# A recurrence kernel on one Trainium2 core: the older wave's products put ahead of the younger wave's in every shared phase

## What is computed

```python
def rwkv7_scan(r, decay, k, v, a, bb, s0):
    def step(s, inp):
        r_t, w_t, k_t, v_t, a_t, b_t = inp
        sa = jnp.einsum('bhij,bhj->bhi', s, a_t)
        s = s * w_t[:, :, None, :] + sa[..., None] * b_t[:, :, None, :] + v_t[..., None] * k_t[:, :, None, :]
        return s, jnp.einsum('bhij,bhj->bhi', s, r_t)
    xs = tuple(jnp.moveaxis(z, 1, 0) for z in (r, decay, k, v, a, bb))
    s, ys = lax.scan(step, s0, xs)
    return jnp.moveaxis(ys, 0, 1), s
```

## Time and profile before

| | us |
|---|---|
| median of three runs | 3079.1 |
| lowest, highest | 3076.35, 3082.09 |
| profiled execution, its time | 3077.25 |
| profiled execution, its span | 3075.1 |
| PE busy | 2827.9 |
| DVE busy | 1222.3 |
| POOL busy | 811.9 |
| ACT busy | 753.4 |

### The profile page before, as it was taken

How to read it: one execution, slowest core, us unless ns; L and a number is a source line. 1 busy time by engine, 2 the same in 40 slices (tenths; PEclk the granted TensorE clock), 3 DMA queues, 4 the chain that set the end, 5 groups by cost and what they waited for, 6 DMA issues and landing times.

```text
span 3075.1 us, 58817 instructions
## 1 busy us (share of the span) xinstructions
PE 2827.9 (92%) x24335; PEld 2689.7 (87%) x24335; DVE 1222.3 (40%) x2402; ACT 753.4 (24%) x1371; POOL 811.9 (26%) x575
## 2 busy tenths in 40 slices
PE   4997777877999999999999999798989999999996
PEld 4997566765799999999999999676989999999996
DVE  6117666675513222121123599974232211121123
ACT  2001344334513121121112310256131111121211
POOL 3212000000162223232236422110532322232345
PEclk9998899998999999999999999899999999999998
DMA  4694000000211111111111211200311111111112
GB/s 123 65 68 54 2 3 3 4 3 20 80 41 38 45 48 40 50 41 43 46 46 36 108 48 41 94 1 4 103 36 36 52 44 45 48 36 53 41 40 74
DMA packets 54003, 138.68 MB, mean 45 GB/s; under 512 B 7248, under 2 KB 23248, under 8 KB 53584
## 3 DMA queue, kind: packets, MB, share of 16 engines
q1 hardware_dynamic: 53840, 136.31, 17.9%
HBM read 119.71 MB, written 16.59 MB: 44 GB/s over the span
## 4 chain that ended last, share of the span: by engine, by line
PE 87%; DVE 8%; ACT 2%; issue 2%; DMA 1%; SPq 0%; ACTq 0%; DVEq 0%; POOLq 0%; POOL 0%
PE PS L319 24%; PE PS L321 24%; PE PS L320 24%; PE PS L1436 3%; PE PS L1387 2%; PE PS L882 1%; PE PS L1462 1%; PE PS L985 1%; DVE zc L1614 1%; PE PS L997 1%; PE PS L935 1%; DVE xx L1316 1%; DVE c_s L1537 1%; DVE h_lo L455 1%; PE PS L1000 1%
## 5 line engine op out<-in xcount | busy, mean ns | idle before, releaser
L319 PE MATMUL PS<-h_hi,w_hi 128*128 128x384 f32 (+1 forms) x3456 | 1135.0, 328 | 63.8 <-POOL w_lo L411 26.3
L320 PE MATMUL PS<-h_lo,w_hi 128*128 128x384 f32 (+1 forms) x3456 | 1132.8, 328 | 0.0
L321 PE MATMUL PS<-h_hi,w_lo 128*128 128x384 f32 (+1 forms) x3456 | 1132.6, 328 | 0.0
L411 POOL TENSOR_TENSOR w_lo<-w_raw,w_hi 128x1024 fp32r<-128x1024 f32 (+2 forms) x208 | 470.2, 2261 | 1113.3 <-ACT w_hi L389 1113.3
L319 PEld LDWEIGHTS PS<-h_hi,w_hi 128*128 128x128 f32 x3456 | 652.8, 189 | 65.0 <-issue 64.7
L320 PEld LDWEIGHTS PS<-h_lo,w_hi 128*128 128x128 f32 x3456 | 652.6, 189 | 0.3
L321 PEld LDWEIGHTS PS<-h_hi,w_lo 128*128 128x128 f32 x3456 | 652.5, 189 | 0.0
L389 ACT ACTIVATE w_hi<-w_raw 128x1024 fp32r<-128x1024 f32 (+2 forms) x208 | 201.8, 971 | 916.5 <-PE PS L321 880.1
L681 DVE TENSOR_TENSOR x<-PS,x 128x384 f32 (+1 forms) x240 | 128.3, 535 | 556.8 <-PE PS L321 551.4
L321 PE MATMUL PS<-hid_hi,w_lo 128*128 128x384 f32 (+1 forms) x1056 | 346.9, 328 | 0.0
L319 PE MATMUL PS<-hid_hi,w_hi 128*128 128x384 f32 (+1 forms) x1056 | 346.7, 328 | 0.0
(11 more groups left out here) (245 smaller groups left out, 2706.4 us busy)
## 6 DMA issues: line engine op xcount, KB each, us to landing
w_raw<-in_w_gu SPq DMA_DIRECT2D x88, 512.0 KB, 3.5
w_raw<-in_w_d SPq DMA_DIRECT2D x48, 384.0 KB, 3.1
w_raw<-in_w_e SPq DMA_DIRECT2D x20, 512.0 KB, 9.0
w_raw<-in_w_o SPq DMA_DIRECT2D x20, 512.0 KB, 3.5
x<-in_x SPq DMA_DIRECT2D x4, 1536.0 KB, 9.1
x_home<-x SPq DMA_DIRECT2D x1, 4352.0 KB, 13.9
w_raw<-in_w_oe SPq DMA_DIRECT2D x8, 512.0 KB, 3.5
w_raw<-in_w_d SPq DMA_DIRECT2D x16, 256.0 KB, 2.7
```

Source lines behind the costliest of these rows:

```text
L319: pe.matmul(out, w_h, a_h, start=k == 0, stop=False)
L320: pe.matmul(out, w_h, a_l, start=False, stop=False)
L321: last = pe.matmul(out, w_l, a_h, start=False, stop=k == kn - 1)
L411: pool.tensor_tensor(w_lo[slot][:, 0:kn, :], w_raw[slot][:, 0:kn, :], w_hi[slot][:, 0:kn, :].bitcast(F32), ALU.subtract).then_inc(sm["w_lo ...
```

## The change

In a mixed phase all products of the back half come ahead of the three `intra`, and the transposes are spread between them. PE: `solved` for both heads, `token_major` 0, `effective`, `token_major` 1, `transfer`, `token_major` 2, `inside`, then `intra` 0, 1, 2. DVE: the `wz` copies, the start state, `r_eff`, `m_all`, then the three reads, `bt_level` and `xx`. ACT: two copies of transposed blocks, `h_all`, the third copy. Every instruction is there as often as before and has the same waits; phases with only one half have the order that they had. No transfer is touched.

```diff
@@ rwkv_act, phase
+                def turned(blk):
+                    act.wait_ge(sm["tm_done"], 3 * qf + (blk + 1))
+                    act.activation(tm[front % 2][blk][:, :, :], PS[:, TM_BANKS[blk], :].rearrange("p (a b) -> p a b", a=4),
+                                   ACT.Copy).then_inc(sm["tm_ready"], 1)
+
                 if front is not None:
-                    for blk in range(WAVE):
-                        act.wait_ge(sm["tm_done"], 3 * qf + (blk + 1))
...
+                    turned(0)
+                    turned(1)
...
                                    ACT.Copy).then_inc(sm["hbd_ready"], 1)
+                if front is not None:
+                    turned(2)
@@ rwkv_pe, phase
                     if back is not None:
                         pe.wait_ge(sm["ysb_ready"], 10 * qb + 10)
-                    token_major(m, front, 0)
-                    token_major(m, front, 1)
                 if back is not None:
                     pe.wait_ge(sm["akv_ready"], qb + 1)
                     solved(back, qb, 0)
-                if front is not None:
-                    token_major(m, front, 2)
-                if back is not None:
                     solved(back, qb, 1)
                 if front is None and m + 1 < PAIRS:
                     decay_low(m + 1)
                 if front is not None:
-                    pe.wait_ge(sm["tm_ready"], 3 * qf + 2)
-                    intra(front, 0)
+                    token_major(m, front, 0)
                 if back is not None:
                     pe.wait_ge(sm["wz_ready"], 2 * qb + 2)
                     pe.wait_ge(sm["y_stored"], qb + 1)
                     effective(back, qb)
                 if front is not None:
-                    pe.wait_ge(sm["tm_ready"], 3 * qf + 3)
-                    intra(front, 1)
+                    token_major(m, front, 1)
                 if back is not None:
                     transfer(back, qb)
                 if front is None and m + 1 < PAIRS:
                     rate_low(m + 1)
                 if front is not None:
-                    pe.wait_ge(sm["sa_ready"], 3 * qf + 1)
-                    intra(front, 2)
+                    token_major(m, front, 2)
                 if back is not None:
                     pe.wait_ge(sm["r_ready"], qb + 1)
                     inside(back, qb)
+                if front is not None:
+                    pe.wait_ge(sm["tm_ready"], 3 * qf + 2)
+                    intra(front, 0)
+                    pe.wait_ge(sm["tm_ready"], 3 * qf + 3)
+                    intra(front, 1)
+                    pe.wait_ge(sm["sa_ready"], 3 * qf + 1)
+                    intra(front, 2)
@@ rwkv_dve, phase
                     ins.then_inc(sm["s_init"], 1)
-                if front is not None:
-                    read_intra(0)
-                if back is not None:
                     dve.wait_ge(sm["reff_done"], qb + 1)
...
                     ins.then_inc(sm["r_ready"], 1)
+                    dve.wait_ge(sm["mh_done"], qb + 1)
+                    dve.wait_ge(sm["mdiag_ready"], qb + 1)
+                    dve.wait_ge(sm["hbd_ready"], qb + 1)
+                    dve.tensor_tensor(m_all[:, :, :].rearrange("p (b a) c -> p b a c", a=2),
+                                      PS[:, 4:6, 0:WAVE * HD].rearrange("p a (b c) -> p b a c", c=HD),
+                                      m_diag[:, :, :].rearrange("p (b a) c -> p b a c", a=2), ALU.add)\
+                       .then_inc(sm["mbd_ready"], 1)
                 if front is not None:
+                    read_intra(0)
                     read_intra(1)
                     read_intra(2)
...
-                if back is not None:
-                    dve.wait_ge(sm["mh_done"], qb + 1)
-                    dve.wait_ge(sm["mdiag_ready"], qb + 1)
-                    dve.wait_ge(sm["hbd_ready"], qb + 1)
-                    dve.tensor_tensor(m_all[:, :, :].rearrange("p (b a) c -> p b a c", a=2),
...
```

More of the change, by code:

```diff
@@ L824, in store_y @@
                     ins.then_inc(sm["y_stored"], 1)
+                def turned(blk):
+                    act.wait_ge(sm["tm_done"], 3 * qf + (blk + 1))
+                    act.activation(tm[front % 2][blk][:, :, :], PS[:, TM_BANKS[blk], :].rearrange("p (a b) -> p a b", a=4),
+                                   ACT.Copy).then_inc(sm["tm_ready"], 1)
                 if front is not None:
-                    for blk in range(WAVE):
-                        act.wait_ge(sm["tm_done"], 3 * qf + (blk + 1))
-                        act.activation(tm[front % 2][blk][:, :, :], PS[:, TM_BANKS[blk], :].rearrange("p (a b) -> p a b", a=4),
-                                       ACT.Copy).then_inc(sm["tm_ready"], 1)
+                    turned(0)
+                    turned(1)
                 if front is None and m + 1 < PAIRS:
@@ L1284, in phase @@
                            .then_inc(sm["x_init"], 1)
-                if back is not None:
-                    dve.wait_ge(sm["mh_done"], qb + 1)
-                    dve.wait_ge(sm["mdiag_ready"], qb + 1)
-                    dve.wait_ge(sm["hbd_ready"], qb + 1)
-                    dve.tensor_tensor(m_all[:, :, :].rearrange("p (b a) c -> p b a c", a=2),
-                                      PS[:, 4:6, 0:WAVE * HD].rearrange("p a (b c) -> p b a c", c=HD),
-                                      m_diag[:, :, :].rearrange("p (b a) c -> p b a c", a=2), ALU.add)\
-                       .then_inc(sm["mbd_ready"], 1)
                 if front is None:
```

## The result

The changed kernel is **slower by a quarter of a per cent**: 3087.39 us against 3079.77 us in the median of 11 runs each, ratio 1.0026 with a 95% interval of 1.0018 to 1.0035, or some 5.5 to 10.8 us. I had forecast 12.4 us; the direction, the place and the range held, the size was too large by about 5 us.

What follows compares the result with a forecast made beforehand. The third read's end sets a mixed phase: PE's list bounds it before, DVE's reads after. M1 1.80 times 4 (7.2) plus M2 1.30 times 4 (5.2) gives +12.4, from 3079.1 to 3091.5 us; range 3083 to 3099.

Steps and rivals of the forecast that it cites:

- The place: Mixed phases: the end of DVE's third read sets the phase's end; level 1 starts 3.69 us behind it.
- The start: Phase start on PE: `solved` waits for the last add before it, `effective` follows 2.26 us later, transpose 0 costs nothing.
- PE from `effective` to the first `intra`: Back half on PE: `effective` 0.40, two transposes 0.65 each, `transfer` 1.05, `inside` 0.70; together 3.45 us.
- The reads: DVE's three reads back to back: first 0.92 us after the first `intra` starts, third ends 2.96 later, 1.80 later than before.
- Stalls ahead of the third read: PE waiting for code in mixed phases: 0.2 us in M1, 0.35 in M2; bounds 0 and 1.1.
- The levels: Behind the third read: lists unchanged; only M1 gains 0.20 us, as the stall ending `inside` no longer holds `values_in`.
- rival A: Loss mostly given back: thinner code stalls in the levels and some worth of `m_all`; +5.8 us, 3083; chance 0.16.
- my three signs of being wrong: Mixed phases: `intra` 0 well before 5.95, the 3.69 from read to level 1 shrinking, or issue stalls shrinking in the levels.
- B: Code stalls come whole, with `transfer` and `inside` run without `intra` between them; slower, 3098 us; chance 0.07.
- C: Faster: PE's density is what mixed phases pay for and the reads hide anyway; -8.2 us, 3071; chance 0.04.
- D: Order doesn't matter: arrival of code sets the end of the front half in both orders; 3079 us; chance 0.04.
- E: Clock falls to 1.2 GHz, slowing PE from `effective` to the first `intra`; 14 us on top, 3105; chance 0.03.

Runs made afterwards that it cites:

- first_intra_earlier: Changed kernel with `intra` 0 of a mixed phase pulled up on PE, between `transfer` and transpose 2: ratio 1.0008 to the kernel before.
- the extra read: Second read of each mixed phase done once more: ratio to the kernel before 1.0042 in the changed kernel, 0.9993 in the kernel before.
- the shifted kernel: Changed kernel with 64 more transposes on PE, once, early in the recurrence, so code pieces end half a piece elsewhere: ratio 1.0020.
- The shifted pair of kernels: Kernel before and changed kernel, each with 64 more transposes on PE early in the recurrence: ratios 0.9986 and 1.0020.
- the shift: Kernel before with 64 more transposes on PE, once, in a wait early in the recurrence: ratio 0.9986.

## Why the prediction was right, and where its size was off

**The place.** Level 0 starts from the third read in both kernels: the first add follows it by 2.99 us wherever neither a stall nor a lower clock lies between. `first_intra_earlier` and the extra read moved that end and the phase with it.

**The start.** `solved` starts at 456.71 - 456.21 = 0.50, expected 0.54; `effective` 2.27 after it, expected 2.26. Transpose 0 cost nothing, as said.

**PE from `effective` to the first `intra`.** 462.62 - 458.98 = 3.64, expected 3.45. Each change between transposes and products costs a gap of about 0.1 (the last products of `transfer` start at 461.05 and the transpose behind them at 461.28, where one group of eight products follows the other by 0.12), and I had counted too few: `transfer` began 1.09 after `effective` (expected 1.05), `inside` 1.80 after `transfer` (expected 1.70), the first `intra` 0.75 after `inside` (expected 0.70).

**The reads.** 0.92 from the start of the first `intra`, then 1.99 and 0.96: expected 0.92, 2.00 and 0.96. The third ends at 10.28, expected 10.10 without stalls.

**Stalls ahead of the third read.** Expected 0.2 in M1 and 0.35 in M2; there are none, the third read ends within 0.01 us in all eight phases. The gaps of 0.19 that I missed stood in for them, so the sum up to the third reads (13.2 expected, 12.4 measured) is right partly by luck. In the shifted kernel two phases do have them.

**The levels: the term that was mis-sized.** I took -0.8 for them (the residue in level 0 of M1) and they gave 5.1. The residue was there: in M1 the first add came 0.45, 0.14, 0 and 0.24 late before and at 2.99 after. The other 4.3 lie behind the first add. Waits for issue in the levels fell from 4.9 to 1.3, which is 3.6 of them; the other 0.7 no row explains. That is the half of rival A that I had argued against; `m_all`, its other half, is worth nothing. One of my three signs of being wrong, stalls for issue that shrink in the levels, came true.

I had argued that code is asked for at the same places of the list and so nothing changes. The places in the list behind the third read did stay; what moved is the time of the fetches. Counted from the end of the third read, they show it in M1. The fetch that started 2.2 us after that end before the change (the same one, by count) starts 0.4 to 1.0 ahead of it now, where PE still waits for the last read. The next fetch starts 4.7 to 5.2 after it instead of 5.6 to 6.2, so the code of the levels is there sooner. M1 gave back 3.8 of the 5.1. In M2 the fetch nearest to the third read's end starts ahead of it in both orders, the next one 2.3 to 3.7 after it instead of 2.6 to 3.4, and M2 gave back only 1.3. The shifted pair of kernels gives back 3.9, and with the third read earlier the rest grows by 6.0. That the stalls are code is shown by the shift and by the fetches; that the earlier fetches are what shortened the levels agrees with these times, but no run tests it by itself.

**The size, and luck.** By the runs the change costs 8.0 us, below the 10 to 16 to which I gave 0.66, and between that and rival A's +5.8. The forecast with the stall half of A taken off is 12.4 - 4.4 = 8.0. So the range held because it took in the upper part of A, and not because the levels had been read rightly.

**The rivals.** B did not come: the pauses were enough. C and D are against the three reads: PE's density was paid for in part, as C says, but the third read was later by 1.98 in M1 and by some 1.1 in M2. E did not come in the changed kernel, but it came with one more read, and in three phases with the first `intra` moved up.

## What to carry to other kernels

Two engines that hand small tiles to each other are paced by the last hand-over, not by the fuller engine: before moving a group of products together, lay the reads of their results end to end and see what is left to hide them. A span with dense small products can be paced by the arrival of its own code; a gain ahead of such a place comes back as a stall behind it, and a loss is partly given back. Where that is so, compare two orders at two places of the code's pieces before believing a few us.

## What the runs showed of the hardware

Sixty-four transposes, put into a wait, moved stalls of 0.4 to 1.2 us from one phase to the other; the whole kernel moved by a ratio of 0.9986, of which the mixed phases explain a third. PE went on 1.21 to 1.60 us after the fetch of a 16 KB piece of code had ended, in each of 92 stalls. TensorE at the 2.4 GHz level went through a phase with waits of 0.42 and 1.09 us without falling; with one wait of 1.22 to 1.29 it fell to the 1.2 GHz level in three phases of eight, and with waits of 0.42 and 1.70 in seven of eight, where 24 products of 64 x 64 took up to 1.55 us instead of 0.92.
